# Experts of a mixture-of-experts layer in order of rank, in place of an interleaved order, in a one-core Trainium2 kernel

## The reference, cut to what matters

```python
scores = sigmoid(x @ w_router)
g_sel = argmax over groups of the sum of the group's two best (scores + bias)
local = the two best experts in that group;  gate = scores of the two, normed to 1
hid = silu(xb @ w1[e]) * (xb @ w3[e])        # per expert, for the tokens that chose it
y[tok] += gate * (hid @ w2[e])
x = layer_norm(ALPHA * x + y)
```

## Time and profile before

| | |
|---|---|
| median of three runs | 2941.3 us |
| lowest and highest | 2939.56 and 2942.33 us |
| the profiled execution | 2942.84 us |
| its span, first to last instruction | 2941.0 us |
| PE busy | 2457.3 us, 84% |
| DVE, ACT, POOL busy | 688.6, 368.3, 67.9 us |
| mean granted PE clock | 0.924 of full |
| bytes moved | 433.22 MB, 147 GB/s over the span |

### The profile page before, as it was taken

How to read it: one execution, slowest core, us unless ns; L and a number is a source line. 1 busy time by engine, 2 the same in 40 slices (tenths; PEclk the granted TensorE clock), 3 DMA queues, 4 the chain that set the end, 5 groups by cost and what they waited for, 6 DMA issues and landing times.

```text
span 2941.0 us, 23888 instructions
## 1 busy us (share of the span) xinstructions
PE 2457.3 (84%) x9176; PEld 1496.2 (51%) x9176; DVE 688.6 (23%) x1352; ACT 368.3 (13%) x798; POOL 67.9 (2%) x82
## 2 busy tenths in 40 slices
PE   2999999969657788996998687999769986689977
PEld 1444433445536557853787555334348875343333
DVE  1010111041555311101122433112122124311212
ACT  1000000010312201001022101010012121110101
POOL 0000000000203000000000000000000000000000
PEclk9999999989778798998999797999989997899998
DMA  9221256313111033434431115787663212068783
GB/s 327 71 86 57 86 196 226 135 43 118 55 57 58 0 109 98 148 117 145 151 115 58 43 58 196 296 346 297 246 197 142 92 54 72 10 267 347 286 340 145
DMA packets 170715, 433.22 MB, mean 147 GB/s; under 512 B 15344, under 2 KB 70896, under 8 KB 151152
## 3 DMA queue, kind: packets, MB, share of 16 engines
q1 hardware_dynamic: 162432, 415.51, 38.3%
q10 hardware_dynamic: 8176, 16.23, 1.5%
HBM read 430.68 MB, written 1.05 MB: 147 GB/s over the span
## 4 chain that ended last, share of the span: by engine, by line
issue 58%; PE 32%; DMA 4%; DVE 3%; ACT 1%; POOL 1%; DVEq 1%; POOLq 0%; SPq 0%; ACTq 0%
PE bank L2665 8%; PE bank L2108 7%; PE bank L2699 4%; PE bank L2667 3%; DMA ring<-in_l_moe_in 2%; PE bank L2373 2%; DMA slot<-in_l_moe_in 2%; PE bank L2701 1%; PE bank L2714 1%; PE bank L2615 1%; PE bank L2223 1%; PE bank L2177 1%; PE bank L2187 0%; PE bank L2195 0%; POOL arena L1245 0%
## 5 line engine op out<-in xcount | busy, mean ns | idle before, releaser
L2108 PE MATMUL bank<-HT,ring 128*128 128x256 f32 (+1 forms) x3392 | 932.2, 435 | 34.7 <-ACT arena L1113 20.7
L2108 PEld LDWEIGHTS bank<-HT,ring 128*128 128x128 f32 x3392 | 644.8, 192 | 316.0 <-issue 225.5
L2134 PE MATMUL bank<-ring,arena 128*128 128x512 f32 x528 | 234.4, 604 | 4.7 <-DMA ring<-in_ffn_w_out 2.7
L2134 PEld LDWEIGHTS bank<-ring,arena 128*128 128x128 f32 x528 | 101.3, 194 | 136.0 <-issue 129.9
L2665 PE MATMUL bank<-ring,TOKENS 128*128 128x512 f32 x352 | 158.3, 594 | 4.3 <-DMA ring<-in_l_moe_in 3.4
L2038 DVE SCALAR_TENSOR_TENSOR tmp<-th,bank 128x256 f32<-128x256 f32 x50 | 21.1, 422 | 453.3 <-ACT th L1205 453.3
L2108 PE MATMUL bank<-arena,ring 128*128 128x256 f32 x448 | 104.8, 396 | 4.4 <-issue 2.3
L2665 PEld LDWEIGHTS bank<-ring,TOKENS 128*128 128x128 f32 x352 | 64.5, 190 | 77.9 <-issue 74.2
L2665 PE MATMUL bank<-slot,TOKENS 128*128 128x512 f32 x160 | 77.0, 626 | 27.5 <-DMA slot<-in_l_moe_in 26.6
L2108 PEld LDWEIGHTS bank<-arena,ring 128*128 128x128 f32 x448 | 88.2, 199 | 21.0 <-issue 7.2
L1080 ACT ACTIVATE arena<-bank 128x256 f32<-128x256 f32 (+2 forms) x78 | 34.5, 450 | 486.5 <-PE bank L2678 343.3
(11 more groups left out here) (408 smaller groups left out, 2254.4 us busy)
## 6 DMA issues: line engine op xcount, KB each, us to landing
ring<-in_l_moe_in SPq DMA_DIRECT2D x42, 2048.0 KB, 11.7
ring<-in_ffn_w_in SPq DMA_DIRECT2D x44, 1024.0 KB, 7.5
ring<-in_w_ada SPq DMA_DIRECT2D x18, 2048.0 KB, 14.5
ring<-in_l_w_gate SPq DMA_DIRECT2D x16, 2048.0 KB, 7.6
ring<-in_l_moe_out SPq DMA_DIRECT2D x14, 2048.0 KB, 8.3
slot<-in_l_moe_in SPq DMA_DIRECT2D x14, 2048.0 KB, 10.2
ring<-in_mix_w_in SPq DMA_DIRECT2D x10, 2048.0 KB, 8.0
ring<-in_ffn_w_out SPq DMA_DIRECT2D x8, 2048.0 KB, 7.9
```

The lines of the kernel that those rows point to most:

```text
L2108: last = mm(out, w[:, k0 + k, c0:c0 + P], rhs(k), start=k == 0, stop=k == kn - 1)
L2134: last = mm(PS[job[0]][:, :], HID[:, f, t * P:t * P + P], w[:, f - part * 8, :], start=f == 0, stop=f == FT - 1)
```

## The change

The order of `expert_order` becomes rank 0, 1, 2 (twelve whole experts), then the eight pairs of ranks 3 to 6, then the four of rank 7. The table of banks is written anew to fit that order. Nothing else differs.

```diff
-    for e in range(PER_GROUP):
-        whole(0, e)
+    for rank in range(3):
+        for e in range(PER_GROUP):
+            whole(rank, e)
+    for rank in range(3, 7):
         for j in range(2):
-            pair(3 + e, j)
-    for e in range(PER_GROUP):
-        whole(1, e)
+            pair(rank, j)
     four(7)
-    for e in range(PER_GROUP):
-        whole(2, e)
     return units, hidden
...
-        DOWN_BANKS = ((2, 3), (4, 5), (2, 3), (6, 7), (6, 7), (6, 7), (6, 7), (6, 7), (4, 5))
+        DOWN_BANKS = ((2, 3), (4, 5), (2, 3), (4, 5), (6, 7), (2, 3), (6, 7), (2, 3), (4, 5))
```

## The result

The changed kernel takes 2957.39 us in the median of 5 runs (2954.63 to 2961.34) against 2941.3 us; the ratio is 1.0056 with a 95% interval of 1.0041 to 1.007. Run again later it gave 1.0039 (1.0021 to 1.0057) and 1.004 (1.0025 to 1.0054). So it is slower, by 0.4 to 0.6%, and inside the range of the forecast, whose value was 2950.0 us.

The account below looks back on a forecast made before the run. TensorE was busy for 84%, and in the expert stage neither it nor the transfers had much to spare. Per pass 324.2 us at full clock plus 4.0 for the clock made 328.2, together +8.8: 2950.0 us, range 2937 to 2970.

Parts of the forecast that it names:

- (a): Front of each expert stage, TensorE bound: no waits for loads, first pair at 170.4 us, last whole down done at 182.7.
- (b): From load 30 on, transfers set the pace: 23 loads of 2 MB at 5.03 us each, load 53 landing at 307.0.
- (c): Stage's end: load 54's slot is freed only after the last pair's down; TensorE waits about 7 us, load lands 316.0.
- (e): Lower clock near the stage's end: 4.0 us per pass, 1.7 ahead of load 54's release, 2.3 for final down and scatters.
- (d): Tail from last down to last scatter: 7.3 us plus 0.9 for a half scatter, giving 324.2 us at full clock.
- (f): New bank table in the expert stage: costs nothing; without cover, one scatter (1.9 us) would be the price.
- no change: Rival, chance 0.25: clock falls only at the last wait (1.6 us), loads come 4.95 us apart; +0.4 in all, 2942.
- the ring: Rival case, chance 0.03: the ring of load slots hides the order of experts, so the change does nothing; 2941 us.
- clock down through the whole end: Rival, chance 0.12: lower clock throughout the stage's end costs 9.7 us, 333.9 per pass, 2962 in all.
- transfers slower when pulled without a break: Rival, chance 0.05: the 23 loads behind load 30 run at 354 GB/s, costing 20.5 us per pass, 2991 in all.
- faster: Rival, chance 0.05: the 23 loads take 4.80 us each and the clock never falls; 318.3 us per pass, 2930 in all.

Follow-up runs that it names:

- the half loads: The changed kernel with the pairs' two in loads cut to half their columns (1 MB per load in place of 2): 2938.2 us, ratio to before 0.9981.
- after_keep_busy: The changed kernel with matmuls of no use added in the waits of the stage's end: 2949.2 us, ratio to before 1.0019.

## Why the prediction was right, point by point

The median came out 7.4 us above the forecast (2957.4 against 2950.0), inside its range and on its side. The stages were forecast at +8.8 us and found at +8.2 in the means of three profiles; what the sum lacked lies outside the stages. That the stages agree to 0.6 us is in part luck: the tail was taken 1.2 us too short, and the clock ahead of load 54 was charged 1.7 us that only one pass of six paid. By its steps, in the first stage of the first profile, times from the first up at 1826.44:

- **(a) Front.** Forecast: first pair at 170.4 us and the last whole's down done at 182.7, no waits. Found: 170.6; load 30, which waits for that down, was issued at 2009.35 - 1826.44 = 182.9. Right.
- **(b) Transfers.** Forecast: load 30 lands 8.2 us after its issue, load 53 at 307.0, 5.03 us per 2 MB. Found: 8.2; load 53 was issued at 2114.41 and landed 18.8 us later, at 306.8. Over the 23 loads behind load 30, which landed at 191.1, that is 5.03 us each, and 5.03 to 5.08 in the other passes. Most landings are 4.93 to 4.99 us apart; one of 5.7 to 6.1 in each pass and some six of 5.0 to 5.6, most of them the four's, raise the mean. The wait per pair was mis-sized: 2.9 us per pair forecast, 2.3 to 2.9 in two pairs found. From the fourth pair on the pairs start 15.5 and 14.3 us apart in turn, 14.9 in the mean, for 15.1. TensorE was taken to need 12.2 us per pair, and it needs 13.6 on average, since every second pair step holds a station's scatter and takes 15.0; the forecast left these scatters out. It changed nothing, as the transfers still set the pace (13.6 is less than 15.1), which the half loads showed.
- **(c) The late slot.** Forecast at full clock: load 54 issued at 308.4 and landed at 316.0; with the 1.7 us of (e) ahead of it 310.1 and 317.7. Found: 309.35 and 316.9 in this pass, after a wait of 5.95 us (about 7 forecast); 307.8 to 308.3 and 315.4 to 315.9 in the other five, which is the forecast at full clock. The down moved ahead took 3.5 to 5.0 us off this landing, so the step is shown and not only argued.
- **(d) Tail.** 8.2 us forecast from the last down to the last scatter, 9.4 found at full clock (second pass of after_keep_busy). This term was 1.2 us short. It was read from the end of the order before, and half a scatter was added. In the new order the four's result also waits for the scatter of the last pairs (the 1.51 us of the rows above), a reading of the rows that no run tested by itself.
- **(e) Clock.** 4.0 us forecast. Behind the load's landing it cost 12.25 - 9.4 = 2.8 us (2143.70 to 2155.95 against that pass), and 2.1 to 2.3 in the other five, whose tails take 11.5 to 11.7 us; 2.3 stood for it. Ahead of the release the four's last quarter lost 3.03 - 1.92 = 1.1 and the pair's down 4.01 - 3.65 = 0.4, together 1.5, for which 1.7 stood. That held for this pass alone: in the other five the last quarter took 1.92 us and the pair's down 3.65, and the clock fell at the two quarters before, where the waits for loads hid it. So the clock cost 4.3 us here and 2.1 to 2.3 elsewhere. Keeping TensorE busy won 1.0 and 2.3 us of it net, the 2.3 in the pass in which the clock stayed up. The last stretch by the forecast: 317.7 + 8.2 + 2.3 = 328.2; as found: 316.9 to the landing, 0.4 to the first matmul of the down, 12.25: 329.5. In a usual pass it is 315.6, 0.4 and 11.6: 327.6.
- **(f) Banks.** No up or down in the timeline waits for a bank.
- **The sum.** 328.2 us per pass against 329.5 and 327.5; difference to before +8.8 forecast, +8.2 in the means. What the sum didn't hold is time outside the stages: +9 us in the first pair of profiles and +5.6 in the means of three. I had taken it as equal because the code is; 3.9 of the 5.6 us had arisen before the first expert load was issued.

Of the rivals, *no change* needed the clock to fall only at the last wait and loads 4.95 us apart, and had neither; the ring didn't hide the order, since the pairs waited for loads; *clock down through the whole end* didn't come: of the four's quarters half or more ran in 1.92 us each, the others in up to 3.5, and the pair's down took 3.65 us, and 4.01 once; *transfers slower when pulled without a break* is refuted by 420 GB/s over 90 us; *faster* needed loads below 4.87 us apart, and they came 5.03 apart.

The Trainium skill ("DMA: Bandwidth & Descriptors", section Specifications) has an HBM limit of about 358 GB/s per core. The 420 GB/s of this kernel, which runs on one core alone, doesn't agree with it. The Trainium skill ("TensorE: Matmul & The Clock Gate", section on HAM oscillation) describes a kernel in which every group of matmuls behind a wait for a transfer starts at the lower level of the clock. Here the trace agrees in part: in the first stage a wait of 2.33 us was followed by half clock (the window at 2097.91) and those of 1.91 and 2.29 us were not, the pair behind each taking 3.65 us.

## What to carry to other kernels

With a ring of few slots, an order of work balances compute and transfer only within the ring's reach: put work that gives transfer time back next to work that needs it, and what lacks it last only where nothing stands behind it. A load queue that is served in order turns one slot that is let go late into a wait of everything behind it, so look for the slot whose release stands in the program behind a use of later loads, and move that release ahead. When two orders are compared, date each stage from its own first instruction; time outside the stages can move by as much as the effect.

## What the runs showed of the hardware

- Queued loads of 2 MB landed 5.03 us apart in the mean over 23 loads (420 GB/s over 90 us), while load 54, alone in the queue, took 7.4 to 7.9 us from issue to landing in six passes. Issued only once the load ahead had landed, it landed 8.6 to 10.1 us behind it; with its slot let go early it landed 4.9 us behind it.
- The time outside the stages, with the same instructions, lay between 2292.4 and 2304.1 us in the thirteen profiles; stretches of matmuls there ran at half clock in one execution and at the full clock in another. That spread, 11.7 us, is larger than the effect of the change in the stages, 8.2.
- Against that a stage repeats closely: the sum of the two came to 646.4 to 648.9 us in three profiles of the kernel before, and to 655.0 to 657.0 in three of the changed one.
- Where the clock falls differs between passes of one kernel, and so does its price: at half clock in the four's last quarter it delayed load 54 by some 1.5 us (one pass of six), and in the quarters before it was hidden by waits for loads.
